# Order of VectorE's and ScalarE's queues at the fronts and at the entries of the output projections, and 64 stationary columns in the widest score level

## What is computed

```python
def swiglu_ffn(h, w_in, w_out):
    gate, up = jnp.split(h @ w_in, 2, axis=-1)
    return (jax.nn.silu(gate) * up) @ w_out

f = swiglu_ffn(rms_norm(x, ffn1_pre_g), ffn1_w_in, ffn1_w_out)
x = x + 0.5 * rms_norm(f, ffn1_post_g)
m = token_mixer(rms_norm(x, mix_pre_g), ...)
x = x + rms_norm(m, mix_post_g)
f = swiglu_ffn(rms_norm(x, ffn2_pre_g), ffn2_w_in, ffn2_w_out)
x = x + 0.5 * rms_norm(f, ffn2_post_g)
```

## Time and profile before

| | |
|---|---|
| median of 3 runs | 2402.92 us (2401.53 to 2403.98) |
| the profiled execution | 2401.99 us, its span 2400.2 us |
| mean granted TensorE clock | 0.991 |
| busy: TensorE, VectorE, ScalarE, GpSimd | 97%, 65%, 35%, 34% |

### The profile page before, as it was taken

The page is one execution under the profiler, slowest core; times in us unless marked ns, Lnnn a source line. Parts: engine busy times, 40 slices in busy tenths (PEclk is TensorE's granted clock), DMA queues, the critical chain, the costliest instruction groups (busy, mean ns, idle before and its releaser), DMA issues. The chain is left out here.

```text
span 2400.2 us, 31100 instructions
## 1 busy us (share of the span) xinstructions
PE 2328.3 (97%) x10995; PEld 1948.0 (81%) x10995; DVE 1565.9 (65%) x1973; ACT 846.0 (35%) x1213; POOL 807.0 (34%) x550
## 2 busy tenths in 40 slices
PE   6999999999989999999999999999999999999997
PEld 5888888788868888888888887787788888887886
DVE  6666665677753795686696594742675656657676
ACT  4333333243554324224224222511343333323443
POOL 5555445200422223223213235213455445540012
PEclk9999999999999999999999999999999999999999
DMA  4333433556832123122122135444313323337565
GB/s 144 88 109 96 121 94 104 176 166 215 266 120 53 27 71 97 27 72 90 35 72 80 53 106 200 143 148 132 124 57 105 109 87 109 96 105 250 154 217 212
DMA packets 237636, 283.84 MB, mean 118 GB/s; under 512 B 10997, under 2 KB 164051, under 8 KB 234707
## 3 DMA queue, kind: packets, MB, share of 16 engines
q1 hardware_dynamic: 230995, 269.77, 36.0%
q10 hardware_dynamic: 6528, 12.58, 1.4%
HBM read 209.44 MB, written 72.88 MB: 118 GB/s over the span
## 5 line engine op out<-in xcount | busy, mean ns | idle before, releaser
L648 PE MATMUL PU<-XH,w_h 128*128 128x512 f32 x1008 | 400.3, 397 | 2.8 <-DVE mt L2128 1.1
L650 PE MATMUL PU<-XH,w_l 128*128 128x512 f32 x1008 | 394.2, 391 | 0.0
L649 PE MATMUL PU<-XL,w_h 128*128 128x512 f32 x1008 | 393.5, 390 | 0.0
L2232 POOL TENSOR_TENSOR ws<-pw,ws 128x512 fp32r<-128x512 f32 x176 | 251.4, 1431 | 220.1 <-ACT ws L1212 220.1
L1970 DVE SCALAR_TENSOR_TENSOR PG<-ub,cw,PG 128x512 f32<-128x512 f32 x464 | 308.0, 750 | 6.1 <-issue 6.1
L2227 POOL TENSOR_TENSOR w_l<-w_raw,w_h 128x2048 fp32r<-128x2048 f32 (+1 forms) x40 | 179.6, 4489 | 321.0 <-ACT w_h L1130 321.0
L648 PEld LDWEIGHTS PU<-XH,w_h 128*128 128x128 f32 x1008 | 190.2, 189 | 46.4 <-issue 5.9
L2232 POOL TENSOR_TENSOR ws<-s_sum,ws 128x512 fp32r<-128x512 f32 x126 | 165.3, 1320 | 183.0 <-ACT ws L1212 183.0
L650 PEld LDWEIGHTS PU<-XH,w_l 128*128 128x128 f32 x1008 | 189.8, 188 | 40.3
L649 PEld LDWEIGHTS PU<-XL,w_h 128*128 128x128 f32 x1008 | 190.3, 189 | 38.8 <-issue 0.2
L2278 POOL TENSOR_SCALAR st<-st 128x1 f32<-128x1 f32 (+1 forms) x56 | 22.8, 407 | 555.7 <-ACT junk L1160 198.2
(11 more groups left out here) (320 smaller groups left out, 5395.3 us busy)
## 6 DMA issues: line engine op xcount, KB each, us to landing
pw<-in_ffn_w_in SPq DMA_DIRECT2D x88, 512.0 KB, 5.8
f_raw<-f_d SPq DMA_DIRECT2D x154, 256.0 KB, 3.1
f_raw<-in_ffn_w_out SPq DMA_DIRECT2D x132, 256.0 KB, 4.1
w_raw<-in_w_mix_in SPq DMA_DIRECT2D x50, 512.0 KB, 5.0
f_d<-s_buf SPq DMA_DIRECT2D x22, 1024.0 KB, 5.0
f_d<-hid SPq DMA_DIRECT2D x22, 512.0 KB, 2.6
x_d<-FACC SPq DMA_DIRECT2D x16, 512.0 KB, 3.3
gate_d<-tmp ACTq DMA_DIRECT2D x16, 512.0 KB, 2.8
```

The costliest lines, as they stand in the source:

```text
L648: pe.matmul(dst, hi(k), xh(k), start=(n == 0), stop=False)
L649: pe.matmul(dst, hi(k), xl(k), start=False, stop=False)
L650: last = pe.matmul(dst, lo(k), xh(k), start=False, stop=(n == KT - 1))
L2232: PT(ws[:, i, 1, :, :], form_source(name, par), ws[:, i, 0, :, :], ALU.subtract).then_inc(form_lo, 1)
```

## The change

TensorE issues what it did, in the order it did; in the level lv = 6 its stationary operand is the first 64 of 128 columns. The other edits move entries within the lists of VectorE, ScalarE, GpSimd and SP.

```diff
 # SP: the store of the last sums, from the end of hidden_phase into out_phase
                 store_odd(n, NM - 1)
-                store_sums(n, NM - 1)
...
-                    if l < RAWS + 2:
+                    if l < RAWS + NM:
                         sp.wait_ge(t_sum, summed(n, l - RAWS))
...
                     step_load(n, l, ov)
+                    if l == NM:
+                        store_sums(n, NM - 1)
 # PE: level
-                        last = pe.matmul(GL[:, lv % 2 * 512 + c * P // 2:lv % 2 * 512 + (c + 1) * P // 2],
-                                         R[:, m % 3, tok], right, start=True, stop=True)
+                        left = P if lv < 6 else P // 2
+                        last = pe.matmul(GL[0:left, lv % 2 * 512 + c * P // 2:lv % 2 * 512 + (c + 1) * P // 2],
+                                         R[:, m % 3, c * P:c * P + left], right, start=True, stop=True)
 # ScalarE: front_rest
                 copy_p1(n, 1, 1)
-                front_forms(n, 6, 8)
-                gate0(n, 1, 1)
+                if n:
+                    front_forms(n, 6, 8)
                 x_fill(n, "B12")
                 x_fill(n, "B22")
+                gate0(n, 1, 1)
+                if n == 0:
+                    front_forms(n, 6, 8)
                 front_forms(n, 8, 9)
 # ScalarE: ahead of the second front
-            s1(4), s2(4), s1(5), s2(5), s1(6), s2(6)
-            x_fill(1, "B11", (0, 1))
-            s1(7)
-            x_fill(1, "B11", (2, 3))
+            s1(4), s2(4), s1(5), s2(5), s1(6)
+            x_fill(1, "B11")
+            s2(6), s1(7)
             x_fill(1, "B21")
 # VectorE: hidden_sums gets parts=range(4) and does the parts asked for; hidden_phase
                 hidden_pair(n, FB - 1, 1, True)
-                hidden_sums(n, NM - 1, evens)
 # VectorE: out_phase
-                for l in range(3):
-                    step_sum(n, l)
-                for l in range(2, N_L):
-                    if l + 1 < N_L:
-                        step_sum(n, l + 1)
-                    step_lo(n, l)
+                step_sum(n, 0)
+                step_lo(n, 2)
+                step_sum(n, 1)
+                step_sum(n, 2)
+                for l in range(3, N_L):
+                    if l < NM:
+                        step_lo(n, l)
+                        step_sum(n, l)
+                        if 4 <= l < 8:
+                            hidden_sums(n, NM - 1, (hid[:, 0, 0, :], hid[:, 0, 1, :]), (l - 4,))
+                        if l == NM - 1:
+                            step_sum(n, NM)
+                    else:
+                        if l + 1 < N_L:
+                            step_sum(n, l + 1)
+                        step_lo(n, l)
 # VectorE: front_rest
-                sums(n, 1, 1, 0)
+                if n:
+                    sums(n, 1, 1, 0)
+                x_rest(n, "B12")
+                x_rest(n, "B22")
                 whole_hidden(n, 0)
                 take(n, 1, 1, "C11")
-                x_rest(n, "B12")
-                x_rest(n, "B22")
+                if n == 0:
+                    sums(n, 1, 1, 0)
 # VectorE: ahead of the second front
-            mix_drain(1, 2), pre(5, 1), post(6, 1), pre(6, 1)
+            mix_drain(1, 2), pre(5, 1), post(6, 1)
             mix_drain(1, 3)
             x_rest(1, "B11")
+            pre(6, 1)
+            x_rest(1, "B21")
             post(7, 1)
-            x_rest(1, "B21")
             pre(7, 1)
 # GpSimd: front_rest
-                front_forms(n, 6, 7)
+                if n:
+                    front_forms(n, 6, 7)
                 for t in range(4):
                     t3_sum(n, t)
+                if n == 0:
+                    front_forms(n, 6, 7)
                 front_forms(n, 7, 9)
```

More of the change, by code:

```diff
@@ L1775, in hidden_pair, with hidden_sums @@
                 hidden0(n, j, par)
-            def hidden_sums(n, m, e):
+            def hidden_sums(n, m, e, parts=range(4)):
                 e0, e1 = e
@@ L1781, in hidden_sums @@
                 done = 4 * NM * n + 4 * m
[L1782 to L1790, removed]
+                if 0 in parts:
+                    dve.wait_ge(hid_ready, N_H * n + 4 * m + 4)
+                    if n or not isinstance(m, int) or m:
+                        dve.wait_ge(s_stored, 16 * NM * n + 16 * m)
+                    TT_(s_buf[:, 0, :], e0, o0, ALU.add).then_inc(s_part, 1)
+                if 1 in parts:
+                    TT_(s_buf[:, 2, :], e1, e0, ALU.subtract).then_inc(s_part, 1)
+                if 2 in parts:
+                    dve.wait_ge(s_part, done + 1)
+                    TT_(s_buf[:, 1, :], s_buf[:, 0, :], e1, ALU.subtract).then_inc(s_part, 1)
+                if 3 in parts:
+                    dve.wait_ge(s_part, done + 3)
+                    TT_(s_buf[:, 3, :], o1, s_buf[:, 1, :], ALU.subtract).then_inc(s_part, 1)
             def hidden_phase(n):
```

## The result

Median 2379.95 us (2378.88 to 2382.44, 4 runs) against 2402.57 us (2401.53 to 2403.98, 4 runs) of the kernel before: ratio 0.9907, 95% interval 0.989 to 0.9924, 22.6 us faster. Forecast were 2378.6 us in a range of 2375 to 2389. Timed again later it took 2379.84 us against 2403.03: 0.9905 (0.9888 to 0.9921).

The account below looks back on a forecast made before the run. TensorE, busy 97% of the span, was taken as the bound: its work must shrink or its idle time close. Terms 11.4 + 5.3 + 4.6 + 3.0 = 24.3 us off 2402.9 gave 2378.6 us, range 2375 to 2389.

Parts of the forecast that it names:

- (c): First front: GpSimd's forms delay every one of the sums and T2 sums, T1's rests 3 us later; 2381.6 us, chance 0.08.
- The entries: Starts of the two projections: both lose their stall through VectorE's new order and the moved store, 2 x 5.7 = 11.4 us.
- Step 4 is the tight one: Projection entry: its raw buffer must be loaded anew after the first T1 sum; ready at 2180.0, due at 2180.6.
- (a): Projection entries: the raw load becomes the bound, step 4 late by 1.6 us in both projections; 2384.6 us, chance 0.13.
- The first front: B22's transposes start 5.0 us sooner, 0.4 us given back at T2's transposes: 4.6 us, bounds 3.5 and 5.0.
- The second front: B21's transposes 4.1 us sooner, 0.2 for the clock, B12 to B22 worth 1.0: 5.3 us, bounds 4.5 and 6.2.
- The clock term: Second front: the shorter wait left before B21's transposes may slow the clock less; 0.2 us more, bounds 0 and 1.1.
- The level: Widest score level in four heads: loading 128 stationary columns sets the 0.106 us distance; 64 columns save 3.0 us.
- (b): Widest score level costs what it did, as a load has a fixed length whatever its columns; 2381.6 us, chance 0.15.
- (d): Projections slower: above 7.1 us of landing the raw buffer's ring exceeds four steps and TensorE stops; 2438 us, chance 0.02.
- (e): The order was not what held these waits; the releasers named are only the last of several; 2400 us, chance 0.04.

Follow-up runs that it names:

- the changed kernel's other profile: Profile of the changed kernel without edit, timed again beside its variants on one chip: 2379.84 us, span 2377.6 us.
- the experiment on the order alone: Kernel before with only VectorE's new `out_phase` order, the four `s_buf` sums and 1 MB store left in place: 2399.18 us in a single run.
- third kernel: Changed kernel with `step_lo` 11 ahead of `step_sum` 12 and, in the first front, the T1 chain ahead of column sums and forms: 2376.79 us.
- three further moves in the fronts: Added in turn: first front's T1 chain first, 2376.79 us; second front's last drain behind `pre` of tile 5, 2376.12; its column sums and forms behind T1, 2374.4.

## Why the prediction was right, and where it was off

The likeliest case came: 2378.6 forecast, 2379.95 measured. Its terms sum to 24.3 us, the same places of the trace to 21.0; in the changed kernel's other profile they come to 22.6, and the medians say 22.6 and 23.2. In the first profile all four terms came out under the forecast. The other differs in the second front, where the clock stayed at 1.00 and the gain was 0.5 us over the forecast: that the total comes so near is in part the luck of that clock. One of the prediction's own signs of being wrong did appear: T2's transposes waited 1.24 us for T1's low part, and over 1 us was the sign of (c).

- **The entries, 11.4: 5.9 and 5.9 measured, as forecast, less 0.7 at step 11.** Of the second entry the chain came out as worked: `step_lo` 2 starts 0.6 us behind the first T1 sum, step 2 on time, clock 1.00. Step 4 is the tight one, as said, and held, so (a) didn't come. In the experiment on the order alone it missed, with the store ahead of its load: that is (a)'s mechanism, at 1.5 us. The slip is in "the load of step 12 queues behind it with more than 8 us to spare". SP's queue in the changed kernel:

```profile
478.13 0.43 SPq L413 DMA_DIRECT2D f_d<-s_buf  x1
...
479.99 1.37 SPq L462 DMA_DIRECT2D f_raw<-in_ffn_w_out  x1
```

  The load was needed at 483.6, when VectorE had `step_sum` 12 next, ahead of `step_lo` 11, and not at step 12. It landed 8 us after its issue, behind 1 MB. So step 11 began 0.6 us late in one profile and 0.2 in the other; the step that failed is that the spare time was counted from step 12's matmuls and not from the queue entry that stands ahead of `step_lo` 11.
- **The first front, 4.6: 3.2 measured.** Up to G01 the gain is 5.0, as worked; then 1.8 are lost where 0.4 were forecast. The column sums were forecast to end at 50.1 and did, at 49.99. The step that failed is the size of the T2 sums behind them: to end at 55.4 they were taken at 1.33 us each (by the prediction's own 1.43 they end at 55.8), and they took 6.88 / 4 = 1.7. The 5.73 us of the earlier trace rows is no price of one sum beside GpSimd: one of those four met GpSimd idle and took 0.68, the other three took 1.75 to 1.77. In the changed kernel GpSimd's two forms, moved behind its T3 sums, fill the gap and all four are held. T1's rests began at 56.79. This is rival (c)'s mechanism at about half its price. The third kernel shows the cure: sums that nobody needs yet must stand behind the ones that somebody waits for.
- **The second front, 5.3: 4.5 measured, 5.8 in the other profile.** Forecast was that B21's transposes start 3.6 us after B11's; it was 4.03, since VectorE's last half of `post` began 0.87 us behind B11's start, not 0.46 as in the earlier trace rows. So the start of these transposes gained 3.6 and not 4.1, and B12 to B22 0.8 and not 1.0. The clock term, the gain from a shorter slow stretch, was taken at 0.2 in bounds of 0 and 1.1; it was 0.1 in the profiled execution, where the clock fell again, and 1.4 in the other, where it didn't: outside its bounds. The moves of tiles 6 and 7 hid, as worked. What was not seen is that `post` of tile 6, 2.5 us, could also have gone behind the drain.
- **The level, 3.0: 2.2 measured, 2.4 by the medians.** That the load of 128 columns set the distance was right, and (b), with its fixed load, is refuted: 1.70 us became 1.08. The distance inside the level came down to the moving side as worked, 0.058 us for 0.054, and that alone would give 2.8 us over four heads. What the sum put at nothing without a reason is the change of width: 0.09 us ahead of the level and 0.07 behind it, 0.6 in all. The Trainium skill (TensorE: Matmul & The Clock Gate, section LDWEIGHTS) gives P / 1.2 ns for P columns, an estimate of 53 ns for 64; the 0.106 us of 128 agrees. For 64 no row here shows it: the measured 0.058 us is near it, but with 32 columns it stays at 0.056, so it isn't the load that is measured. The table at the head of the same page, by which the stationary operand is always 128x128, doesn't agree with this measurement.
- **(d) and (e)** didn't come. Steps 2 to 10 start without a wait in both projections, step 11 in the second, and every wait that the change was aimed at went when the releaser named came sooner.

## What to carry to other kernels

A TensorE wait on one named queue is worth its length plus the clock it costs, and the cure is to sort that queue by due times: what an engine makes early for a later stage belongs behind the first thing that somebody waits for, on every engine and in the DMA queue, or the next entry of the list becomes the wait. After each move read the rows again: of three further moves in the fronts two took 1.85 and 1.3 us, and the one between them paid only when the sums behind it had moved too. Price VectorE sums with both operands in SBUF one by one, by whether GpSimd is in an operation when they begin, and not by a mean over a group. Price narrower stationary operands only down to the distance that the moving columns allow, and put down something for each change of width.

## What was not expected of the hardware

- **VectorE beside GpSimd.** Four T2 sums of 128x512 took 6.88 us in the changed kernel's first front, 5.73 before, 4.67 in the third kernel. Their mean is no price: a single sum is either free or held. The rows are one sum and the GpSimd operation beside it in the changed kernel, then the first and the third sum and the T4 sum beside the third in the third kernel:

```profile
49.99 1.77 DVE L1694 TENSOR_TENSOR FACC<-FACC 128x512 f32<-128x512 f32 x1
49.48 1.73 POOL L2253 TENSOR_TENSOR ws<-s_sum,ws 128x512 fp32r<-128x512 f32 x1
```
```profile
46.46 0.68 DVE L1695 TENSOR_TENSOR FACC<-FACC 128x512 f32<-128x512 f32 x1
47.66 1.77 DVE L1695 TENSOR_TENSOR FACC<-FACC 128x512 f32<-128x512 f32 x1
...
47.22 1.67 POOL L2275 TENSOR_TENSOR FACC<-FACC 128x512 f32<-128x512 f32 x1 [0.91 <-DVE FACC L1695]
```

  A sum that begins while GpSimd is in an operation ends 0.55 us after that operation; otherwise it takes 0.68. Of the changed kernel's 107 VectorE operations of this form with both operands in SBUF that began so, 103 ended 0.54 to 0.56 us after the GpSimd operation, whether that was a form or a sum. The 93 that read an operand from PSUM took 0.68 to 0.69 beside GpSimd too. The groups of four differ in how many were held: four in the changed kernel, three before, two in the third kernel.
- **The clock** fell to 0.83 behind waits of 2.13, 2.23 and 2.77 us ahead of B21's transposes and not behind 2.19 and 2.52 us. The spread of a kernel's runs goes with it only in part: the changed kernel's four spans were 2377.1 twice at a mean clock of 0.994, 2379.2 at 0.992 and 2380.6 at 0.993.
- **A change of the stationary width** inside a stream of matmuls cost 0.09 us at the first narrow one and 0.07 behind the last, in all four heads of each of the five traces read for it (64 columns in four, 32 in one).
